# x's token-major form by VectorE and DMA, its tiles convolved first, and state products in three rounded parts

## The reference

```
zxbcdt = h @ w_in                                # z, x, B, C and dt
xbc = silu(causal_dwconv(xbc, conv_w, conv_b))   # 4 taps along the tokens
dt = softplus(dt_raw + dt_bias)
# 4 groups of 8 heads of 64 channels; 4 chunks of 128 tokens
xdt = x * dt[..., None]
y_diag = einsum("bcgls,bcgrls,bcsgrp->bclgrp", C @ B^T, decay, xdt)
states = einsum("bclgn,bcgrl,bclgrp->bcgrpn", B, decay_to_end, xdt)
# scan over the chunks: state = state * chunk_decay + states
y_off  = einsum("bclgn,bcgrpn,bcgrl->bclgrp", C, prev_state, exp(a_cs))
y = y_diag + y_off + d_skip * x                  # then silu(z) gate, group norm, w_out
```

## Time and profile before

| | us |
|---|---|
| median of 3 runs | 1107.36 (1107.17 to 1107.75) |
| the profiled execution's own time | 1107.1 |
| its span, first to last instruction | 1105.3 |
| PE busy | 1093.8 (99%) |
| POOL, DVE, ACT busy | 593.3 (54%), 570.3 (52%), 468.5 (42%) |
| mean granted TensorE clock | 0.998 |

### The profile page before, as it was taken

One profiled execution on the slowest core, in us unless ns is written; L12 is line 12 of the kernel. 1 busy time (PEld: TensorE's weight loads), 2 busy tenths in 40 slices (PEclk: granted clock), 3 DMA queues, 4 the chain that ended last, 5 costly groups with the idle time before them and its releaser, 6 DMA issues.

```text
span 1105.3 us, 15325 instructions
## 1 busy us (share of the span) xinstructions
PE 1093.8 (99%) x5156; PEld 898.0 (81%) x5156; DVE 570.3 (52%) x640; ACT 468.5 (42%) x804; POOL 593.3 (54%) x448
## 2 busy tenths in 40 slices
PE   9999999999999999999999999999999999999997
PEld 7788888888888788788788878888888888888886
DVE  5665421455423284666777856666664224554123
ACT  7433222233333338558595774343332222333332
POOL 3766544444565635337364474656665444445653
PEclk9999999999999999999999999999999999999999
DMA  7223232222222225333324333222222222323232
GB/s 286 83 99 103 89 101 96 95 95 95 95 95 95 95 77 156 126 105 124 130 92 141 122 107 106 96 95 95 95 95 95 95 95 95 98 99 101 93 104 77
DMA packets 40085, 117.05 MB, mean 106 GB/s; under 512 B 4080, under 2 KB 11888, under 8 KB 40048
## 3 DMA queue, kind: packets, MB, share of 16 engines
q1 hardware_dynamic: 39616, 115.83, 31.3%
q10 hardware_dynamic: 432, 0.73, 0.2%
HBM read 114.32 MB, written 2.23 MB: 105 GB/s over the span
## 4 chain that ended last, share of the span: by engine, by line
PE 97%; DMA 1%; DVE 1%; POOL 1%; issue 0%; ACT 0%; ACTq 0%; DVEq 0%; POOLq 0%
PE bank L832 30%; PE bank L833 30%; PE bank L834 30%; PE bank L1023 1%; PE bank L1032 1%; PE bank L1040 1%; DMA params<-params 1%; PE bank L982 1%; PE bank L873 1%; POOL residual L739 0%; PE bank L1000 0%; PE bank L853 0%; PE bank L961 0%; PE bank L991 0%; DVE residual L1223 0%
## 5 line engine op out<-in xcount | busy, mean ns | idle before, releaser
L712 POOL TENSOR_TENSOR w_lo<-w_raw,w_hi 128x512 fp32r<-128x512 f32 x372 | 499.4, 1348 | 464.2 <-ACT w_hi L437 451.8
L437 ACT ACTIVATE w_hi<-w_raw 128x512 fp32r<-128x512 f32 x372 | 230.6, 626 | 403.9 <-PE bank L834 397.7
L832 PE MATMUL bank<-x_hi,w_hi 128*128 128x512 f32 x848 | 336.1, 396 | 1.7 <-DVE x_lo L1133 1.5
L834 PE MATMUL bank<-x_hi,w_lo 128*128 128x512 f32 x848 | 330.6, 390 | 0.0
L833 PE MATMUL bank<-x_lo,w_hi 128*128 128x512 f32 x848 | 330.5, 390 | 0.0
L832 PE MATMUL bank<-act_hi,w_hi 128*128 128x512 f32 (+1 forms) x656 | 254.5, 388 | 0.0
L834 PE MATMUL bank<-act_hi,w_lo 128*128 128x512 f32 (+1 forms) x656 | 252.2, 384 | 0.0
L833 PE MATMUL bank<-act_lo,w_hi 128*128 128x512 f32 (+1 forms) x656 | 252.1, 384 | 0.0
L832 PEld LDWEIGHTS bank<-x_hi,w_hi 128*128 128x128 f32 x848 | 159.3, 188 | 39.2 <-issue 4.9
L833 PEld LDWEIGHTS bank<-x_lo,w_hi 128*128 128x128 f32 x848 | 159.4, 188 | 34.1 <-issue 2.1
L834 PEld LDWEIGHTS bank<-x_hi,w_lo 128*128 128x128 f32 x848 | 159.3, 188 | 33.3
(11 more groups left out here) (154 smaller groups left out, 683.4 us busy)
## 6 DMA issues: line engine op xcount, KB each, us to landing
w_raw<-weights SPq DMA_DIRECT2D x186, 512.0 KB, 3.3
m<-acs_scratch SPq DMA_DIRECT2D x16, 512.0 KB, 4.4
decay_in<-eacs_scratch SPq DMA_DIRECT2D x24, 128.0 KB, 3.7
x_token<-x_tok SPq DMA_DIRECT2D x4, 512.0 KB, 6.3
residual<-xt SPq DMA_DIRECT2D x8, 256.0 KB, 9.9
out_first<-scaled_residual SPq DMA_DIRECT2D x4, 256.0 KB, 2.4
out_second<-output_rows SPq DMA_DIRECT2D x4, 256.0 KB, 2.7
pooling_matrices<-pooling ACTq DMA_DIRECT2D x2, 288.0 KB, 5.1
```

The lines of the kernel that those rows point to most:

```text
L437: act.activation(whi[:, c % 2, part], raw[:, c % 2, part], ACT.Copy).then_inc(hi_ready, 1)
L712: pool.tensor_tensor(wlo[:, c % 2, part], raw[:, c % 2, part], whi_f[:, c % 2, part], ALU.subtract).then_inc(lo_ready, 1)
L832: pe.matmul(out, wh, xh, start=start, stop=False)
L834: return pe.matmul(out, wl, xh, start=False, stop=stop)
```

## The change

1. The order of a group's convolved tiles becomes x0 to x3, B, C (before: B, C, x0 to x3). `conv_out`, `silu_b_c` and the host's order of the weights follow. `silu_x` moves to t = 8 of the group before (for group 0: between the units 4 and 5).
2. PE's 16 transposes of x per group go. DVE transposes blocks of 32 x 32 into the place where y will be (`transpose_blocks`, 4 instructions, at t = 9 of the group before), SP writes them to DRAM with 4 DMAs of 256 KB and rows of 512 bytes (`write_blocks`) and reads them back at t = 0 as one DMA of 1 MB with rows of 2 KB (`read_tokens`).
3. `x_dt` is then made by DVE from SBUF instead of PSUM, in two instructions of 256 columns for each chunk. `skip`, which overwrites that place, moves from t = 0 to t = 3 and waits for all of `x_dt`.
4. The state product becomes three rounded products: `b_token_hi` (ACT), `b_token_lo` (DVE), `x_dt_decayed_hi` (ACT, `decayed_hi`), `x_dt_decayed_lo` (POOL, `decayed_lo`). With one buffer for the decayed x, chunk 0's stands at t = 2 (now ahead of `group_sum`), chunk 1's at t = 4 and chunk 2's at t = 6.
5. On DVE m of chunk 3 stands ahead of `after_chunk` of chunk 2 at t = 8.

```diff
# SP
+            def write_blocks(g):
+                sp.wait_ge(xt_blocks, g + 1)
+                blocks = x_blocks(g)
+                for a in range(P // Q):
+                    sp.dma_start(x_dram[g, :, :, a, :].rearrange("n q f -> q n f"),
+                                 blocks[Q * a:Q * a + Q, :, :]).then_inc(xt_written, 16)
+            def read_tokens(g):
+                sp.wait_ge(xt_written, 16 * (P // Q) * (g + 1))
+                sp.dma_start(yx[:, GT * g:GT * g + GT, :],
+                             x_dram[g].rearrange("(c b) q a f -> (b q) c (a f)", c=CHUNKS)
+                             ).then_inc(xt_landed, 16)
             load_ahead(5)
+            write_blocks(0)
             sp.wait_ge(scratch, 2 * GROUPS * 16)
...
                     load_ahead(slot_of(g, t))
+                    if t == PER_GROUP - 1 and g + 1 < GROUPS:
+                        write_blocks(g + 1)
+                    if t == 0:
+                        read_tokens(g)
# ACT
+                if u == 4:
+                    silu_x(0)
...
+            def decayed_hi(g, c):
+                act.wait_ge(dec_ready, 3 * g + c + 1)
+                act.activation(dec_hi[:, :], dec[:, :], ACT.Copy).then_inc(dec_hi_ready, 1)
...
+                    if t == 2:
+                        decayed_hi(g, 0)
                     ahead(u, 0)
                     if t == 0:
                         silu_b_c(g)
-                        silu_x(g)
...
+                    if t in (4, 6):
+                        decayed_hi(g, (t - 2) // 2)
+                    if not ends and t == 8:
+                        silu_x(g + 1)
-                    if t == 0:
+                    if t == 3:
                         skip(g)
# POOL
+            def decayed_lo(g, c):
+                pool.wait_ge(dec_hi_ready, 3 * g + c + 1)
+                pool.tensor_tensor(dec_lo[:, :], dec[:, :], dec_hi_f[:, :], ALU.subtract).then_inc(dec_lo_ready, 1)
...
+                    if t == 2:
+                        decayed(g, 0)
                     if t == 2 and g:
                         group_sum(g - 1)
                     if t == 2:
-                        decayed(g, 0)
-                        decayed(g, 1)
+                        decayed_lo(g, 0)
                     split_half(U_SSM + u + 2, 0)
# PE
-                for c in range(CHUNKS - 1):
-                    token_x(g, c)
...
-                    pe.matmul(b_st[:, :], bt[:, c, :], dec[:, c % 2, :], start=True, stop=True).then_inc(st_ready, 1)
+                    three(b_st[:, :], bt_hi[:, c, :], bt_lo[:, c, :], dec_hi[:, :], dec_lo[:, :], True, True
+                          ).then_inc(st_ready, 1)
# DVE
+            def transpose_blocks(g):
+                dve.wait_ge(x_act, g + 1)
+                blocks = x_blocks(g)
+                for i in range(GT):
+                    last = dve.transpose(blocks[:, :, Q * i:Q * i + Q],
+                                         xact[:, i, :].rearrange("p (n j) -> p n j", j=Q))
+                last.then_inc(xt_blocks, 1)
...
                         token_x(g, 0)
                         token_x(g, 1)
                         token_x(g, 2)
-                    if t == 3:
-                        token_x(g, 3)
+                        b_token_lo(g)
+                    if t == 8:
+                        decay_times_cb(g, TIMES_CB_IN[t])
```

More of the change, by code:

```diff
@@ L566, in first_tap, with silu_x @@
                                ).then_inc(tap_ready, 1)
+            def silu_x(g):
+                act.wait_ge(acc_drained, A_SSM + conv_slot(CONVS * g + GT - 1) + 1)
+                act.activation(xact[:, :, :], xact[:, :, :], ACT.Silu).then_inc(x_act, 1)
             for u in range(CONVS):
@@ L809, in _ @@
                     split_half(U_SSM + u + 2, 1)
-                    if CHUNK_AFTER.get(t - 1) == 0:
-                        decayed(g, 2)
+                    if t in (4, 6):
+                        decayed_lo(g, (t - 2) // 2)
                     if g == GROUPS - 1 and t == 10:
@@ L977, in _ @@
                     cumulate()
-            def token_x(g, c):
-                for i in range(GT):
-                    last = pe.transpose(XT_BANK[c][:, P * i:P * i + P], xact[:, i, P * c:P * c + P], ident)
-                last.then_inc(x_mm, 1)
             def token_major(g):
@@ L1019, in chunk @@
                 pe.wait_ge(xdt_ready, 4 * g + c + 1)
-                if c:
+                if g == 0 and c == 0:
+                    pe.wait_ge(acsf_ready, 1)
+                else:
                     pe.wait_ge(y_add, 4 * g + c)
@@ L1319, in token_x, with b_token_lo @@
             def token_x(g, c):
-                dve.wait_ge(x_mm, 4 * g + c + 1)
-                dve.tensor_tensor(by_head(xdt[:, c, :]), by_head(XT_BANK[c][:, :]),
-                                  of_group(dt_t[:, :, :].rearrange("p c h -> p (c h)"), c, g, HD), ALU.mult
-                                  ).then_inc(xdt_ready, 1)
+                dve.wait_ge(xt_landed, 16 * (g + 1))
+                if g and c == 0:
+                    dve.wait_ge(yd_ready, 4 * g)
+                    dve.wait_ge(dec_ready, 3 * g)
+                out = xdt[:, c, :].rearrange("p (i h a j) -> p h i a j", h=2, a=2, j=Q)
+                landed = yx[:, GT * g + c, :].rearrange("p (h a i j) -> p h i a j", h=2, a=2, j=Q)
+                dt = dt_t[:, c, HPG * g:HPG * g + HPG].rearrange("p (i h) -> p h i", h=2)
+                for half in range(2):
+                    last = dve.tensor_tensor(out[:, half], landed[:, half],
+                                             dt[:, half].unsqueeze(2).unsqueeze(3).to_broadcast([P, GT, 2, Q]),
+                                             ALU.mult)
+                last.then_inc(xdt_ready, 1)
+            def b_token_lo(g):
+                dve.wait_ge(bt_ready, g + 1)
+                dve.tensor_tensor(bt_lo[:, :, :], b_misc[:, 0:P * (CHUNKS - 1)].rearrange("p (c n) -> p c n", n=P),
+                                  bt_hi_f[:, 0:CHUNKS - 1, :], ALU.subtract).then_inc(bt_lo_ready, 1)
             def decay_times_cb(g, c):
@@ L1425, in _ @@
                         after_chunk(g - 1, CHUNKS - 1)
+                    if t == PER_GROUP - 1 and not ends:
+                        transpose_blocks(g + 1)
                     if t == 1 and g:
```

77 lines of the change are left out of this document (42 added, 35 removed).

## The result

The changed kernel takes 1130.67 us (median of five runs, 1128.79 to 1132.09), the kernel before 1107.36 (1107.15 to 1107.75): ratio 1.021, 95% interval 1.0198 to 1.0221. It is slower by 23.3 us, where 4.2 were forecast and 1118 was the upper end of the range. The sign was right, the size was not. The profiled execution took 1128.79 us, with a span of 1127.0.

A forecast was written before the change was run, and what follows sets the result against it. PE was taken as the bound, busy 1093.8 of 1105.3 us. The sum was 1107.1 - 9.0 (PE's savings) + 6.5 (group 0) + 1.0 (clock) + 2.3 + 3.7 (later passages) = 1111.6 us, range 1102 to 1118.

The forecast's parts named there:

- What PE saves: On PE, dropped transposes of x save 7.0 us and 12 cheaper state products 2.0, together 9.0 us.
- Group 0: Ahead of chunk 0 of group 0, PE waits 6.5 us (3.5 to 7.7) for m, behind the read of x.
- the step on SP and the read: In group 0, SP issues the read of x at 434.9 us; it lands between 439.3 and 443.5.
- The clock: Behind group 0's wait, PE's first matmuls run at half rate, costing 1.0 us (bounds nothing and 5.6).
- Group 0 to 1: At the passage from group 0 to 1, DVE's slack covers the transposes, so PE does not wait.
- Groups 1 to 2 and 2 to 3: At these passages PE waits 2.3 us (0.5 to 4) and 3.7 us (0.5 to 6).
- the step that priced x_dt: On DVE, the six halves of x_dt take 2.0 us.
- third rival: x_dt's halves each wait for a POOL instruction, taking 5 us or so instead of 2.0: 1117 us, chance 0.10.
- m of chunk 3: The edit that moves m of chunk 3 on DVE costs nothing, since PE did not wait for it.
- The second: Transfers stay under cover at group 0, whose wait and clock loss fall out: 1104.1 us, or 1098 to 1102; chance 0.27.
- The fourth: Gains and waits cancel: group 0 waits 4 us, no clock lost, passages 1.5 and 3: 1106.6 us, chance 0.20.
- first rival: PE starves at chunk 0 of groups 0, 2 and 3: 1111.6 us (1109.6 to 1118), chance 0.43.

The follow-up runs named there:

- one_early_psum_tr: Changed kernel with the read of x early, x_dt from PSUM, no DVE transposes in groups 1 to 3, and one float32 state product: 1105.54 us.
- read_early: Changed kernel with SP's read of x straight behind the writes in group 0 and ahead of the weights load in groups 1 to 3: 1122.26 us.
- one_state: Changed kernel with the one float32 state product and POOL's earlier order back, x's new path kept: 1126.65 us.
- early_psum: Changed kernel with read_early's SP order and x_dt as one product per chunk from a PSUM bank (values of x left out): 1119.85 us.
- early_psum_tr: early_psum without DVE's transposes in groups 1 to 3, x_conv written as it is: 1116.63 us.
- parts_only: Kernel before with only the three-part state product, its roundings and POOL's order for them; m's order unchanged: 1108.14 us.
- parts_m3: Kernel before with the three-part state product and m of chunk 3 ahead of DVE's additions of chunk 2: 1106.71 us.
- m_mid: Changed kernel with read_early's SP order and m of chunk 0 ahead of x_dt of chunks 1 and 2 on DVE: 1125.90 us.
- m_first: Changed kernel with group 0's loads of m issued ahead of the four writes of x: 1128.51 us.
- xdt_plain: Changed kernel with x_dt as one product of 512 contiguous columns per chunk, from SBUF (channel order left out): 1133.00 us.
- xdt_psum: Changed kernel with x_dt as one plain product per chunk from a PSUM bank (values of x left out): 1128.95 us.

## Why the prediction was wrong, step by step

**What PE saves, 9.0: right.** The chunks' distance fell by 0.18 us (forecast 0.17), and where nothing waits (one_early_psum_tr, with its one product) chunk 0 of group 2 follows that of group 1 at 66.5 us in place of 68.3, 1.8 less (forecast 1.75).

**Group 0, 6.5 us (3.5 to 7.7): the step on SP and the read failed; 11.6.** The first half came out as written: tap and taps, transposes of 0.6 us each (2.41), done at 427.7 (forecast 427.2), m's Exp ended at 443.0 (441.7). Then I took issue times from a quiet queue. The loads of m took 2.6 us to issue in place of 0.8 and the weights 1.4, so the read went out at 438.0 in place of 434.9. It took 9.25 us where I had 8.6 for the saturated case, and landed at 447.3. Behind it x_dt took 2.95, not 2.0. read_early shows that it is the place in SP's order: 4 us sooner issued, 8 us sooner there.

**The clock, 1.0: mis-sized and put at one place only; 5.4.** The direction was right, as was my remark that 6.5 us reach the low level. But waits of 5 us at groups 2 and 3 reach it too, and the low level then lasts over the first 3 to 5 us of work, which I could not read from the earlier trace rows.

**Group 0 to 1, nothing: wrong; 1.0, and 0.6 for w_lo.** In the same group 0.9 for m of chunk 2 comes on top, a wait that one_state does not have. The cover was there and was used up: the gate no longer waits for Silu of z, but lies beside POOL's w_lo and takes 5.78 us in place of 3.60, and then DVE waits 1.7 us for x's landing and does x_dt in 5.16.

**Groups 1 to 2 and 2 to 3, 2.3 and 3.7: the step that priced x_dt failed; 5.0 and 5.1, besides the clock.** Six halves were costed at 2.0 us and took 5.09. My own third rival had this price (5 us, from the ratio of the earlier trace rows), and I gave it 0.10 while the text said that rule and trace agreed. What the parts are worth in PE's waits at the two groups shows from run to run: the early read takes 0.7 and 0.0 off, x_dt as one product from PSUM 1.3 and 1.5 more (read_early to early_psum), leaving out the transposes 2.4 and 3.0 more (early_psum_tr). So x_dt's 2.9 and the landing's 0.7 are most of the 4.1 us that my two terms were short; the transposes were priced right and were in the sum. I took my wait from POOL's chain, as the later one by 1.2 us. The lo did end 1.1 us behind m (594.7 against 593.6), with 2.26 us in place of 1.3, but PE wants it only behind chunk 0's product, and all of the 10.1 us of wait end with m.

**m of chunk 3, nothing: right in that PE does not wait for it.** parts_only against parts_m3 shows what it is worth with the three parts: 1.4 us.

**Rivals.** The second, everything under cover, is refuted at group 0 by 11.6 us. The fourth fell with it. The sum of the first rival's mechanism and the third's was what happened. I had treated them as alternatives, though they act one behind the other on the same instruction, and had let the range end where only one of them was true.

**Together.** Group 0 was 5.1 us short, the clock 4.4, group 1 2.5, and groups 2 and 3 4.1. That is 16.1 of the 19.1 us between forecast and measurement; 1.9 more is the distance of the profiled execution from the median, and some 1 us is left without an account.

What stays open is how group 0 could be covered: even with the read straight behind the writes PE waits 4.2 us there (in m_mid 1.7 for m and 2.2 for w_lo), and no run here moved the transposes ahead. The new order of the tiles and the early Silu of x, which make the exponentials end 2.9 us later at group 0 (422.3 against 419.4), were never run alone.

## What to carry to other kernels

When a result that was early becomes one that comes at the last moment, price everything that hangs behind it again, including chains that the trace shows as covered: here the same three-part product cost 0.8, 4 or some 11 us, by how much of its chain other late chains covered. When two chains end at one instruction within a microsecond, shortening one says little of its cost; take both away. And where a text finds that a trace supports a surcharge (here two SBUF inputs beside POOL), that surcharge belongs in the sum, not among the rivals.

## What the runs showed of the hardware that was not expected

- Behind other transfers SP's issue itself gets slower: a write of 256 KB went from 0.31 us for the first to 1.24 for the fourth, two loads of m took 0.81 us to issue before and in m_first, where they stand ahead of the writes, and 2.59 behind them.
- The low clock outlasts the wait: the records show 0.50 up to 5 us behind PE's restart at group 2, and that adds 2.5 us to a wait of 5.0. In all runs here a single wait of about 5 us cost 1.6 to 3.0 us more in this way, and two short ones with 2 us of work between them (xdt_plain, 2.7 and 2.1 us) 3.7 at group 2 and 2.2 at group 3. That two are dearer than one is not shown, as the ranges overlap.
- A DVE transpose of 128 x 512 float32 in blocks of 32 takes 0.60 us in a row of four (2.41), no more than a product from PSUM.
- Making x_dt cheap moved part of the surcharge to the next product with two SBUF inputs, as POOL was still busy: m went from 1.23 to 2.14 us at group 2 (xdt_psum), and from 1.22 to 2.03 at group 0 (read_early to early_psum).
